# Expert chunks of a mixture-of-experts backbone: PE turns replaced by DVE block transpositions, plain copies on ACT, stores issued by Pool

## What is computed

```python
he = jax.nn.silu(t @ w_gate[e]) * (t @ w_up[e])      # [tokens, 512]
y = y + gates[:, e:e + 1] * (he @ w_down[e])         # [tokens, 1024]
```

## Time and profile before

| | |
|---|---|
| median of 3 runs | 1245.73 us (1242.93 to 1247.1) |
| profiled execution | 1249.11 us, span 1247.4 us |
| granted PE clock, mean | 0.906 |
| PE / ACT / DVE busy | 955.2 / 363.0 / 418.5 us |
| bytes moved by DMA | 326.56 MB |

### The profile page before, as it was taken

How to read it: one execution, slowest core, us unless ns; L and a number is a source line. 1 busy time by engine, 2 the same in 40 slices (tenths; PEclk the granted TensorE clock), 3 DMA queues, 4 the chain that set the end, 5 groups by cost and what they waited for, 6 DMA issues and landing times.

```text
span 1247.4 us, 23521 instructions
## 1 busy us (share of the span) xinstructions
PE 955.2 (77%) x9105; PEld 549.4 (44%) x9106; DVE 418.5 (34%) x1124; ACT 363.0 (29%) x744; POOL 66.2 (5%) x106
## 2 busy tenths in 40 slices
PE   5799989989962887888888836998993755556883
PEld 3244554433442443444444415785573422323542
DVE  1366655663143111111111217568624100100112
ACT  3322355552031122222222215227612111110221
POOL 0000000000002000000000020000001000000001
PEclk9899999998966998999999976999996977887995
DMA  9999398797033298896989957005045799999942
GB/s 327 403 354 320 134 387 315 272 337 270 0 135 143 75 337 298 325 361 248 398 302 398 367 204 272 1 19 202 1 145 201 274 396 395 395 393 396 397 174 105
DMA packets 139502, 326.56 MB, mean 262 GB/s; under 512 B 9456, under 2 KB 18048, under 8 KB 139456
## 3 DMA queue, kind: packets, MB, share of 16 engines
q1 hardware_dynamic: 118064, 294.36, 63.4%
q0 software_dynamic: 7200, 22.81, 5.2%
q10 hardware_dynamic: 14192, 8.76, 2.3%
HBM read 308.99 MB, written 33.69 MB: 275 GB/s over the span
## 4 chain that ended last, share of the span: by engine, by line
PE 40%; DMA 12%; SPq 10%; ACT 8%; issue 7%; DVE 6%; ACTq 5%; POOL 1%; DVEq 1%; POOLq 0%
SPq L280 9%; PE bank L592 7%; PE bank L524 7%; PE bank L572 5%; ACTq L823 4%; DMA h_t<-h_rows 4%; PE bank L424 4%; PE bank L494 3%; DMA y_rows<-work 3%; ACT L817 3%; PE bank L367 3%; PE bank L465 2%; DMA ring<-in_w_up_dram 2%; PE bank L477 2%; PE bank L535 1%
## 5 line engine op out<-in xcount | busy, mean ns | idle before, releaser
L572 PE MATMUL bank<-ring,h_t 128*32 128x256 f32 x4160 | 259.1, 405 | 68.8 <-DMA ring<-in_w_up_dram 58.7
L572 PEld LDWEIGHTS bank<-ring,h_t 128*32 128x32 f32 x4160 | 140.9, 117 | 173.5 <-issue 103.8
L592 PE MATMUL bank<-ring,h_t 128*32 128x256 f32 x2080 | 130.7, 393 | 21.5 <-issue 16.2
L817 ACT ACT_TABLE_LOAD x65 | 83.4, 1283 | 154.8 <-issue 145.1
L424 PE MATMUL bank<-h_t,ring 128*128 128x512 f32 (+1 forms) x320 | 118.1, 524 | 12.3 <-ACT h_t L732 12.3
L1157 DVE TENSOR_TENSOR h_t<-h_t,bank 128x128 f32<-128x128 f32 x65 | 18.7, 288 | 257.3 <-ACT h_t L817 257.3
L1154 DVE COPY h_t<-bank 128x256 f32<-128x256 f32 x65 | 27.6, 425 | 213.1 <-PE bank L572 209.6
L563 PE MATMUL bank<-cst,h_t 128*128 128x128 f32 x134 | 29.8, 304 | 87.5 <-DVE h_t L1147 87.5
L592 PEld LDWEIGHTS bank<-ring,h_t 128*32 128x32 f32 x2080 | 66.5, 112 | 65.9 <-issue 31.6
L424 PEld LDWEIGHTS bank<-h_t,ring 128*128 128x128 f32 x320 | 62.5, 196 | 60.7 <-issue 40.9
L524 PE MATMUL bank<-tokm,ring 128*128 128x512 f32 (+1 forms) x256 | 85.3, 496 | 1.0 <-DVE tokm L1019 1.0
(11 more groups left out here) (148 smaller groups left out, 1028.6 us busy)
## 6 DMA issues: line engine op xcount, KB each, us to landing
ring<-in_w_gate_dram SPq DMA_DIRECT2D x32, 2048.0 KB, 13.6
ring<-in_w_up_dram SPq DMA_DIRECT2D x32, 2048.0 KB, 17.4
ring<-in_w_down_dram SPq DMA_DIRECT2D x32, 2048.0 KB, 16.5
ring<-in_ada_w_dram SPq DMA_DIRECT2D x24, 2048.0 KB, 10.1
ring<-in_w_in_dram SPq DMA_DIRECT2D x8, 1536.0 KB, 17.8
h_t<-h_rows POOLq DMA_DIRECT2D x70, 128.0 KB, 5.2
h_rows<-in_table_dram SPq DMA_DIRECT2D x1, 8704.0 KB, 45.0
y_rows<-in_table_dram SPq DMA_DIRECT2D x1, 8704.0 KB, 64.0
```

The costliest lines, as they stand in the source:

```text
L572: last = mm(bank[1][CHUNK * q:CHUNK * q + CHUNK, 0:256], hc_t[:, k, :], w[q // 2][:, k, 256 * (q % 2):256 * (q % 2) + 256], start=(k == 0) ...
L592: last = mm(bank[4][CHUNK * q:CHUNK * q + CHUNK, 0:256], h, wd[:, k, 256 * q:256 * q + 256], start=(k == 0), stop=(k == KF - 1))
L817: do(act_g, turned_he[:, :, 0:2 * CHUNK], ACT.Silu).then_inc(silu_done[l], 1)
```

## The change

- Features of gate and up are interleaved: each column group of PE gets gate features and up features of the same numbers, side by side in the free dimension (`w[:, :, k, :, 32q:32q+32]`), so that silu and product are done where the sums lie in PSUM, with no turn between them.
- The rows are loaded quarter-major (partition 32q + r), and the token rows are written in a permuted order of features beforehand, so that 32x32 block transpositions on DVE give both `hc_t` and `he_t`. All PE turns of the chunks are gone.
- ACT copies out of PSUM with a plain copy instruction in place of an Identity activation, and issues no stores. In layer 0 it does silu(g+1) ahead of the copy out of chunk g.
- Pool issues one store of 128 KB per chunk, in a loop that alternates stores and row loads. `yrow` has two buffers, and row loads run up to four chunks ahead by number.
- The DRAM arrays grow from 2176 to 2304 zeroed rows.

```diff
@@ PE, experts @@
-                def turn_rows(n):
-
-                    pe.wait_ge(hc_moved[l], n + 1)
-                    for j in range(2):
-                        last = turn(bank[5][:, P * j:P * j + P], hc[:, P * j:P * j + P], ident)
-                    last.then_inc(hc_turned[l], 1)
...
-                    w = [ring[:, 3 * a + s, :].rearrange("p (k n) -> p k n", k=KD) for s in range(2)]
+                    w = ring[:, 3 * a:3 * a + 2, :].rearrange("p s (k c m) -> p s k c m", k=KD, c=KF)
                     pe.wait_ge(hc_ready[l], g + 1)
+                    pe.wait_ge(he_ready[l], g + 1)
                     for k in range(KD):
                         for q in range(4):
-                            last = mm(bank[1][CHUNK * q:CHUNK * q + CHUNK, 0:256], hc_t[:, k, :],
-                                      w[q // 2][:, k, 256 * (q % 2):256 * (q % 2) + 256],
+                            o = bank[1][CHUNK * q:CHUNK * q + CHUNK, 0:256]
+                            last = mm(o.rearrange("r (s c i) -> r s c i", s=2, c=KF), hc_t[:, k, :],
+                                      w[:, :, k, :, CHUNK * q:CHUNK * q + CHUNK],
                                       start=(k == 0), stop=(k == KD - 1))
                     last.then_inc(gu_mm[l], 1)
...
                     with pe.Fori(g0 + 1, g1) as g:
                         gate_up(g, a)
-                        turn_rows(g + 1)
+                        weights_in(a, turns, (2,))
                         down(g - 1, a)
-                        turn_he(g)
@@ ACT, experts @@
-                    act.wait_ge(he_turned[l], g + 1)
-                    do(act_g, turned_he[:, :, 0:2 * CHUNK], ACT.Silu).then_inc(silu_done[l], 1)
-                    act.wait_ge(down_mm[l], g + 1)
-                    act.wait_ge(rows_stored[l], 64 * g + 64)
-                    do(yrow, bank[4][:, 0:256], ACT.Identity).then_inc(rows_ready[l], 1)
-                    act.wait_ge(rows_ready[l], g + 2)
-                    for q in range(4):
-                        act.dma_start(y_rows[bass.ds(CHUNK * g, CHUNK), 256 * q:256 * q + 256],
-                                      yrow[CHUNK * q:CHUNK * q + CHUNK, :]).then_inc(rows_stored[l], 16)
+                def gated(g):
+                    act.wait_ge(gu_mm[l], g + 1)
+                    do(act_g, bank[1][:, 0:P], ACT.Silu).then_inc(silu_done[l], 1)
+
+                def row_out(g):
+                    act.wait_ge(down_mm[l], g + 2)
+                    act.wait_ge(rows_stored[l][0], (g + 2) // 2 * 16)
+                    act.wait_ge(rows_stored[l][1], (g + 3) // 2 * 16)
+                    nc.scalar.copy(yrow[:, bass.ds(g % 2 * 256, 256)], bank[4][:, 0:256]).then_inc(rows_ready[l], 1)
...
+                    gated(0)
+                    with act.Fori(0, total - 1) as g:
+                        gated(g + 1)
+                        row_out(g)
+                    row_out(total - 1)
@@ Pool @@
                 with pool.Fori(0, (total + 1) // 2) as m:
                     for i in range(2):
-                        pool.wait_ge(hc_moved[l], 2 * m + 1 + i)
-                        load_rows(2 * m + 2 + i, i)
...
+                        pool.wait_ge(rows_ready[l], 2 * m + 2 + i)
+                        pool.dma_start(y_rows[bass.ds(CHUNK * (2 * m + i), CHUNK), :].rearrange("r (q c) -> q r c", q=4),
+                                       yrow[:, 256 * i:256 * i + 256]).then_inc(rows_stored[l][i], 16)
+                        pool.wait_ge(hc_moved[l], 2 * m + 3 + i)
+                        load_rows(2 * m + 4 + i, i)
@@ DVE, experts @@
                     dve.wait_ge(gu_mm[l], g + 1)
-                    v.tensor_copy(he, bank[1][:, 0:256]).then_inc(he_ready[l], 1)
                     rows_turned(g + 1)
                     dve.wait_ge(silu_done[l], g + 1)
-                    v.tensor_tensor(he_t, act_g, turned_he[:, :, 2 * CHUNK:P], ALU.mult).then_inc(het_ready[l], 1)
+                    v.tensor_tensor(he, act_g, bank[1][:, P:2 * P], ALU.mult).then_inc(he_ready[l], 1)
+                    dve.wait_ge(he_ready[l], g + 2)
+                    dve.wait_ge(down_mm[l], g + 1)
+                    v.transpose(he_t.rearrange("p k r -> p (k r)"), he).then_inc(het_ready[l], 1)
                     rows_in(g + 2)
```

More of the change, by code:

```diff
@@ L286, in refill @@
                 load_expert(l, e + 3, a, (0, 1))
-                sp.wait_ge(down_mm[l], done)
+                sp.wait_ge(down_mm[l], done + 1)
                 load_expert(l, e + 3, a, (2,))
@@ L589, in down @@
                     for k in range(KF):
[L590 removed]
                         for q in range(4):
[L592 removed]
+                            last = mm(bank[4][CHUNK * q:CHUNK * q + CHUNK, 0:256], he_t[:, k, :],
                                       wd[:, k, 256 * q:256 * q + 256], start=(k == 0), stop=(k == KF - 1))
@@ L655, in combine @@
                     tile_sums(nt - 1)
+            for l in range(DEPTH):
+                pe.sem_inc(down_mm[l], 1)
             pe.wait_ge(cst_in, 16)
@@ L808, in route @@
                     act.wait_ge(h_turned, 2 * sum(TOK_TILES[:l]) + q + 1)
-                    do(tokm[:, q // 2, 512 * (q % 2):512 * (q % 2) + 512], bank[2 + q % 4][:, :],
+                    rows = tokm[:, q // 2, :].rearrange("p (j k i) -> p k j i", j=4, k=KD)
+                    do(rows[:, 4 * (q % 2):4 * (q % 2) + 4],
+                       bank[2 + q % 4][:, :].rearrange("p (k j i) -> p k j i", k=4, j=4),
                        ACT.Identity).then_inc(tok_ready, 1)
@@ L869, in _ @@
                 norm_shift(2 * l, 512)
+                if l == 0:
+                    for stored in rows_stored:
+                        act.wait_ge(stored[0], 16)
+                        act.wait_ge(stored[1], 32)
                 qkv(l)
@@ L883, in _ @@
         def _(pool):
-            for l in range(DEPTH):
-                pool.sem_inc(rows_stored[l], 64)
+            pool.wait_ge(block_zeroed, 1)
+            for turns in (1, 2):
+                for l in range(DEPTH):
+                    for i in range(turns - 1, 2):
+                        pool.dma_start(y_rows[ROWS:ROWS + CHUNK, :].rearrange("r (q c) -> q r c", q=4),
+                                       ring[:, 8, 0:256]).then_inc(rows_stored[l][i], 16)
+                        pool.wait_ge(rows_stored[l][i], 16 * turns)
             for l in range(DEPTH):
@@ L907, in load_rows @@
                     pool.dma_start(hc_got[:, 256 * i:256 * i + 256],
-                                   h_rows[bass.ds(CHUNK * n, CHUNK), :].rearrange("r (q c) -> (r q) c", q=4)
+                                   h_rows[bass.ds(CHUNK * n, CHUNK), :].rearrange("r (q c) -> q r c", q=4)
                                    ).then_inc(hc_in[l][i], 16)
-                load_rows(0, 0)
-                load_rows(1, 1)
+                for n in range(4):
+                    if n >= 2:
+                        pool.wait_ge(hc_moved[l], n - 1)
+                    load_rows(n, n % 2)
                 total = all_chunks(pool, l)
@@ L1198, in _ @@
                 dve.sem_inc(rows_ready[l], 1)
+                dve.sem_inc(he_ready[l], 1)
+            v.memset(ring[:, 8, 0:256], 0.0).then_inc(block_zeroed, 1)
             v.memset(eps[:, 0:1], D * EPS)
```

81 lines of the change are left out of this document (39 added, 42 removed).

## The result

The change made the kernel slower, by 1%: 1256.97 us (1253.9 to 1259.89, 4 runs) against 1244.33 (1240.24 to 1247.1, 4 runs) for the kernel before, beside it on the same chip. The ratio is 1.0104, with a 95% interval of 1.0065 to 1.0143. The profiled span is 1254.4 us (before 1247.4), with a mean granted PE clock of 0.883.

The account below looks back on a forecast made before the run. Layer 0 was held by ACT's ring, neither PE nor DMA; layer 1 by weights until 1141. Savings 62.5 + 5 less ends 3.4 and 0.7 give 63.4 us: 1249.1 becomes 1185.7 profiled, median 1182, range 1160 to 1214.

Parts of the forecast that it names:

- ACT's ring is cut and its work is hidden: Layer 0: ACT's 7.52 us cycle per chunk goes; its remaining work runs beside PE's 5.59 us of gate_up and down.
- The refills become the limit: Layer 0: expert weight refills, not PE, set the end; last down at 673 instead of 735.5, 62.5 us saved.
- 91.8 MB at 395 GB/s is 232 us: Layer 0: time to move the refills of 13 experts plus row transfers of about 38 chunks at layer 1's rate.
- 673: Layer 0: forecast end of the last down in us, in place of 735.5.
- Until 1141 weights bound layer 1 and nothing changes: Layer 1: no gain up to 1141 us; only the 10 chunks after it save, 5 us.
- The 1.21 us from gate_up to down: Layer 1, last 10 chunks: path from gate_up to down shortens from 1.72 to 1.21 us, saving 5 us.
- The landing of the row load, 5.3 to 7.2 + 1.3 to 2.6: Row load from issue to landing: 5.3 to 7.2 us, plus 1.3 to 2.6 if on four engines.
- the 9.8: Layer 0: longest landing in us considered for a row load on four engines, giving a chunk period of 6.65 us.
- row transfers set the pace, on four engines: Rival, layer 0: landings up to 9.8 us give period 6.65; 45 us saved, 1200 us in all; chance 0.17.
- The ends: Behind the last chunks: an extra store and load cost 3.4 us in layer 1, one load 0.7 in layer 0.
- 1185.7: Forecast time of the profiled execution in us, from 1249.1; the median was put at 1182.
- DVE waits for rows in most chunks: Sign in the changed profile that would show the forecast wrong: DVE waiting for row loads in most chunks.

Follow-up runs that it names:

- with whole rows: Changed kernel with the DRAM side of Pool's row load and store as 128 outermost pieces of 1 KB, values wrong: 1184.08 us, ratio 0.9525.
- the run with short ends: Changed kernel without loads behind Pool's last stores, DVE's last unused copy, or ACT's wait for stores at the last turn: 1248.75 us, ratio 1.0032.

## Why the prediction was wrong

It said 1182 us, in 1160 to 1214; it is 1257, slower than the kernel before where 62 us less were forecast. Step by step:

- *ACT's ring is cut and its work is hidden*: right. Silu, product and transpositions lie beside PE's work; from 0.2 to 1 us was allowed for the unknown ones, they took 0.31, 0.45 and 0.37. Gate_up did not slow down. The chunk came out at 5.18 us instead of 5.59, since the records of gate_up and down overlap by 0.2 us at each end; as PE was not the limit, this changed nothing.
- *The refills become the limit*: right. The step that failed is its rate: "91.8 MB at 395 GB/s is 232 us". The 395 were read from a stage whose row loads were whole rows. With the loads of the change the full DMA moves 341, and the refills take 20.95 us in place of 17.7. Ten intervals make 33 us of the 39.9 by which the last down of layer 0 missed 673; with whole rows it is at 673.8.
- *Until 1141 weights bound layer 1 and nothing changes*: wrong by the same step. With 371 GB/s instead of 395 it is 11.2 us longer, where 5 less were forecast. The 1.21 us from gate_up to down came as worked out, 1.22 from 1210.62 + 3.64 to 1215.48.
- *The landing of the row load, 5.3 to 7.2 + 1.3 to 2.6*: 9.0 in the median, inside; 11.3 at most, above the 9.8. The working priced four engines in the landing alone and compared it with what the chunk's period hides. What it left out was that the transfer lowers the rate of everything beside it. So the rival "row transfers set the pace, on four engines" had the right pattern and the wrong way: 1200 us by a late landing, 1257 by a slower weights' stream.
- *The ends*: layer 1's cost 8.2 us instead of 3.4, and layer 0's 11.4 instead of 0.7. The loads and waits for chunks that do not exist are 5.0 and 4.8 us of it, as the run with short ends shows (12.7 to 7.7 and 15.9 to 11.1); the other 3.2 and 6.6 stand mostly behind the slower last stores. The working took an idle landing (2.2), where the shortest load of the changed kernel took 3.5. It also counted one load for layer 0 behind the last store; there were two in the stretch, and each had to be copied by DVE before the gather.
- *The sum of the misses*: 39.9 for layer 0, 16.2 for layer 1 (11.2 + 5), 10.7 and 4.8 for the ends make 71.6 us. The profiled execution, 1256.4, missed its 1185.7 by 70.7.
- *The sign "DVE waits for rows in most chunks"* came true (36 waits, 173.7 us), but it tells little: with whole rows DVE waits 89.1 us, and layer 0 ends as forecast.

The Trainium skill (DMA: Bandwidth & Descriptors, Why a DMA increments its semaphore by 16 and not by 1, on how many engines) says that a transfer goes on the largest number of engines, up to 16, that divides the slowest dimensions of both patterns. The count of packets in flight, 8, 12 and 16, agrees with it. What such a load cost the transfers beside it, 13% of the stream (390 to 338 GB/s), the runs alone show.

## What to carry to other kernels

A sustained transfer rate belongs to the mix of patterns it was measured with. Where a change alters the pattern of a small transfer in a stage bound by DMA, price that pattern in the others' rate, not in its own bytes and its own landing: here a load of 0.13 MB per chunk cost some 1.2 us of everybody's stream per chunk ((20.95 - 17.84) / 2.6). Look at the outermost dimension of a load: with 8 pieces half of the loss remained, with 128 none. If the layout needs a small one, split the transfer; that gave back 380 of 394 GB/s here. A long wait beside a full DMA need not be worth anything: halving DVE's wait for rows moved the end of layer 0 by 2 us. And look at what runs behind the last iteration of a loop that prefetches: at two stage ends that was 8 us.

## What the runs showed of the hardware

- Loads with 4 or 2 outermost pieces brought a full DMA from 390 GB/s to 338 and 337, with 8 to 362. A store with four cost 4 GB/s beside whole loads (394 to 390).
- The weights' packets slowed with it (89 to 102 ns for 2 KB), while the busy share stayed at 1.05; a full DMA by its share need not be one at its rate.
- Four small transfers from Pool in place of one big one left 377 to 380 GB/s of 394, also with half as many of them.
- DVE transposed 128x256 in 32x32 blocks in 0.45 us and 128x128 in 0.31. A Pool issue took 0.55 us for a load of whole rows, 0.68 in four quarters, 0.50 for a quarter of it.
